# Input projection of a hybrid attention layer: seven block products in place of eight, rotated channels gathered, weight sums on GpSimd

## The reference, cut to what matters

```python
u = rms_norm(h, pre_norm)                       # (4096, 1024)
proj = einsum('bsd,de->bse', u, w_in)           # w_in: (1024, 3072)
qa, ka, va, ga, qb, kb, vb, gb, qc, gc = split(proj)   # 384,128,128,384, 384,384,384,384, 256,256
qa, ka, qb, kb = rope(...)                      # only the first 16 of each head's 64 channels are rotated
oa = banded_attention(qa, ka, va, sink)         # window 128
ob = three dilated attentions over qb, kb, vb, combined
oc = attention of qc over 256 memory tokens; their keys and values = rms_norm(mem, mem_norm) @ w_mem_kv
y  = concat(oa*silu(ga), ob*silu(gb), oc*silu(gc)) @ w_out
h  = h + rms_norm(y, post_norm)
```

## Time and profile before

| | |
|---|---|
| three runs | 2332.77, 2340.96, 2333.12 us; median 2333.12 |
| span of the profiled execution | 2347.5 us (no time of its own is given beside the span) |
| TensorE busy / VectorE / ScalarE / GpSimd, over the span | 94% / 62% / 51% / 1% |
| first and last matmul of the projection | 57.46 and 1181.96 us |
| first matmul of the attention stage | 1185.67 us |
| HBM traffic | 228 MB read, 131 MB written |

### The profile page before, as it was taken

How to read it: one execution, slowest core, us unless ns; L and a number is a source line. 1 busy time by engine, 2 the same in 40 slices (tenths; PEclk the granted TensorE clock), 3 DMA queues, 4 the chain that set the end, 5 groups by cost and what they waited for, 6 DMA issues and landing times. The chain is left out here.

```text
span 2347.5 us, 41538 instructions
## 1 busy us (share of the span) xinstructions
PE 2209.0 (94%) x13452; PEld 1846.3 (79%) x13452; DVE 1460.4 (62%) x4335; ACT 1208.0 (51%) x3198; POOL 26.3 (1%) x44
## 2 busy tenths in 40 slices
PE   5999999999999999999989999999999888899998
PEld 4888778877888778887878888888777777678886
DVE  4661237603365134641158898888889877788886
ACT  4212551225412353122279899788689878633332
POOL 0000000000000001000100000000000000000000
PEclk9999999999999999999979899899899989999999
DMA  5346434554345545448557867775869876355543
GB/s 189 130 151 186 133 113 143 169 159 140 107 147 171 155 141 192 144 158 232 155 112 132 162 122 138 138 146 113 161 134 214 200 174 184 118 165 169 167 161 125
DMA packets 394645, 361.08 MB, mean 154 GB/s; under 512 B 199120, under 2 KB 324176, under 8 KB 389504
## 3 DMA queue, kind: packets, MB, share of 16 engines
q1 hardware_dynamic: 389648, 337.51, 54.1%
q0 software_dynamic: 4848, 21.71, 3.0%
HBM read 228.34 MB, written 130.81 MB: 153 GB/s over the span
## 5 line engine op out<-in xcount | busy, mean ns | idle before, releaser
L61 PE MATMUL p_ps<-p_uT_hi,p_w_hi 128*128 128x512 f32 x1536 | 603.1, 393 | 2.5 <-DVE p_w_lo L395 2.5
L62 PE MATMUL p_ps<-p_uT_lo,p_w_hi 128*128 128x512 f32 x1536 | 599.3, 390 | 0.0
L63 PE MATMUL p_ps<-p_uT_hi,p_w_lo 128*128 128x512 f32 x1536 | 599.0, 390 | 0.0
L1265 ACT ACTIVATE probs<-probs,a_stat 128x256 f32<-128x256 f32 (+1 forms) x896 | 433.3, 489 | 52.6 <-DVE a_stat L1099 49.4
L395 DVE TENSOR_TENSOR p_w_lo<-p_w_raw,p_w_hi 128x1024 fp32r<-128x1024 f32 x96 | 117.7, 1226 | 382.6 <-ACT p_w_hi L292 363.6
L61 PEld LDWEIGHTS p_ps<-p_uT_hi,p_w_hi 128*128 128x128 f32 x1536 | 289.6, 189 | 62.8 <-issue 2.9
L63 PEld LDWEIGHTS p_ps<-p_uT_hi,p_w_lo 128*128 128x128 f32 x1536 | 289.2, 188 | 60.3
L62 PEld LDWEIGHTS p_ps<-p_uT_lo,p_w_hi 128*128 128x128 f32 x1536 | 289.3, 188 | 59.2
L1099 DVE CUSTOM_DVE_ANT_0 probs<-a_ps_s,fixed 128x256 f32<-128x256 f32 (+1 forms) x704 | 251.3, 396 | 115.1 <-PE a_ps_s L998 112.6
L1052 PE MATMUL a_ps_o<-a_pT,a_v 128*64 128x128 f32 x3320 | 264.1, 291 | 23.5 <-ACT a_pT L1289 22.0
L1068 PE MATMUL a_ps_t<-fixed,probs 128*128 128x128 f32 x1660 | 266.7, 283 | 6.2 <-ACT a_pT L1289 4.3
(11 more groups left out here) (167 smaller groups left out, 2689.2 us busy)
## 6 DMA issues: line engine op xcount, KB each, us to landing
p_w_raw<-in_w_in SPq DMA_DIRECT2D x96, 512.0 KB, 4.0
scratch_qk_hi<-p_o_hi SPq DMA_DIRECT2D x96, 256.0 KB, 2.0
scratch_qk_lo<-p_o_lo SPq DMA_DIRECT2D x96, 256.0 KB, 2.4
a_v<-scratch_v SPq DMA_DIRECT2D x40, 512.0 KB, 7.4
p_x<-in_x SPq DMA_DIRECT2D x32, 512.0 KB, 4.0
scratch_v<-p_o_v SPq DMA_DIRECT2D x256, 64.0 KB, 2.0
scratch_gate<-p_rot SPq DMA_DIRECT2D x64, 256.0 KB, 2.3
a_gate<-scratch_gate SPq DMA_DIRECT2D x64, 256.0 KB, 5.4
```

Source lines behind the costliest of these rows:

```text
L61: nc.tensor.matmul(out, w_hi, m_hi, start=first, stop=False)
L62: nc.tensor.matmul(out, w_hi, m_lo, start=False, stop=False)
L63: return nc.tensor.matmul(out, w_lo, m_hi, start=False, stop=last)
L1265: last = nc.scalar.activation(place, place, ACT.Exp, scale=-1.0, bias=stat[:, s, 0, u.column:u.column + 1], accum_out=stat[:, s, 1, u.colu ...
```

## The change

The projection is now cut in 12 groups per quarter, 48 in all (`PAIRS`). A group is a 2x2 block product: two tiles of 128 channels by two chunks of 512 tokens, with K in two halves of 512. One level of Strassen's scheme, in Winograd's form, makes its four output blocks from 7 products of 4 slices of K by 3 passes, 12 matmuls each, where 8 of that size were needed before. For this

- the token side needs four sums per quarter of 128x2048 (`add_u`), and seven splits in high and low (`high_u`, `low_u`, 128x2048 each) in place of the split of each transposed tile. There is one set of `u_hi` and `u_lo`, which is rewritten while the last group of a quarter still runs;
- the weight side needs four sums per group (`w_added`). GpSimd computes them in the first quarter, they are stored in HBM (`w_s`) and loaded from there in the later ones. Each of the seven blocks of 128x512 is split on ScalarE and VectorE two products ahead (`high_w`, `low_w`), in every quarter;
- of the output side, ScalarE copies two products per group (L477, L482) and VectorE adds twice (`join`); the rest is added up in PSUM. There are 6 banks, three for each of two groups in turn.

The channels are gathered anew: one group (R) and the half of another (L) hold all rotated channels, three groups (P) only plain channels of the same heads, and one (C) the memory queries, two (V) values and four (G) gates. The rows in HBM are as before. The tiles of the next quarter are transposed in groups 2 to 9 of a quarter; ScalarE scales a tile by its root, and the gain is multiplied in while VectorE copies the transposed tile (`keep`). The memory's keys and values are computed inside quarter 3, in its groups 1 to 5. All loops are written out.

```diff
-ORDER = ROPE_TILES + PLAIN_TILES + V_TILES + GATE_TILES
+PAIRS = (("G", 0), ("R", 0), ("G", 1), ("P", 0), ("P", 1), ("P", 2), ("L", 0), ("C", 0), ("V", 0), ("V", 1), ("G", 2), ("G", 3))
...
+        ACT_AT = {"G": (4, 5, 6, 7), "C": (4, 5, 6, 7), "P": (4, 5, 6, 7), "L": (7, 5, 10, 7), "R": (7, 9, 12, 14), "V": (6, 7, 8, 9)}
+        DVE_AT = {"C": (5, 6, 7, 8), "P": (5, 6, 7, 8), "L": (7, 6, 11, 9), "R": (8, 10, 13, 15)}
...
+        def claim_a(eng, n):
+            if n >= 4:
+                g, block = A_AT[n - 4]
+                eng.wait_ge(a_stored[n % 4], stored_before(A_AT, n, 4))
...
+                def high_w(m):                    # ScalarE
+                    g, j = divmod(m, NJ)
+                    if g < NP and j in (1, 2, 4, 5):
+                        act.wait_ge(w_added, 4 * g + {1: 1, 2: 2, 4: 3, 5: 4}[j])
...
+                    if m >= 3:
+                        act.wait_ge(multiplied, m - 2)
+                    nc.scalar.activation(w_hi[:, m % 3, :, :], w_raw[:, entry(j, g), :, :], ACT.Copy).then_inc(w_hi_ready, 1)
...
+                def slot(g, j):                   # ScalarE
+                        if j == 1:
+                            act.wait_ge(multiplied, NJ * g + 1)
...
+                            nc.scalar.activation(ps[:, 3 * (g % 2) + 2, :], ps[:, 3 * (g % 2), :], ACT.Copy).then_inc(products_copied, 1)
...
+                        high_w(m + 2)
+                    if i == NP - 1 and quarter < 3 and j > 0:
+                        high_u(quarter + 1, j - 1)
...
+                keep(XT - 1, front_bank(XT - 1))  # VectorE, ahead of the first group
+                for n in range(3):
+                    add_u(0, n)
+                for j in range(1, NJ):
+                    low_u(0, j)
+                    if j == 3:
+                        add_u(0, 3)
...
+                def slot(g, j):                   # VectorE
+                    if g < G:
+                        if j == 3:
+                            join(g, 0)
+                        if j == 5:
+                            join(g, 1)
+                        low_w(NJ * g + j + 2)
...
+                    if quarter < 3 and i == NP - 2 and j in (1, 2):
+                        add_u(quarter + 1, j - 1)
+                    if quarter < 3 and i == NP - 1 and j > 0:
+                        low_u(quarter + 1, j - 1)
+                        if j == 1:
+                            add_u(quarter + 1, 2)
+                        if j == 4:
+                            add_u(quarter + 1, 3)
...
+                def product(g, j):                # TensorE
+                    if i == 0:
+                        pe.wait_ge(u_lo_ready, NJ * quarter + j + 1)
+                    pe.wait_ge(w_lo_ready, m + 1)
...
+                    if j in (2, 3):
+                        pe.wait_ge(products_copied, 2 * g + 1)
+                    if j in (4, 5):
+                        pe.wait_ge(joined, 2 * g + 1)
+                    if j == 6:
+                        pe.wait_ge(joined, 2 * g + 2)
...
+                for g in range(NP):               # GpSimd
+                    nc.gpsimd.tensor_tensor(s1, a21, a22, ALU.add).then_inc(w_added, 1)
+                    nc.gpsimd.tensor_tensor(s2, s1, a11, ALU.subtract).then_inc(w_added, 1)
+                    nc.gpsimd.tensor_tensor(a21, a11, a21, ALU.subtract).then_inc(w_added, 1)
+                    nc.gpsimd.tensor_tensor(s4, a12, s2, ALU.subtract).then_inc(w_added, 1)
```

More of the change, by code:

```diff
@@ L55 @@
 FIXED = 12 * P
[L56 to L63, removed]
+SWAP = [*range(8, 16), *range(8), *range(24, 32), *range(16, 24)]
 def project_stage(nc, io, sc, early, ahead):
@@ L91, in project_stage @@
[L91 to L101, removed]
+        KH = KD // 2
@@ L114, in project_stage @@
[L114 to L119, removed]
@@ L127, in project_stage @@
[L127 to L138, removed]
@@ L140, in pairs @@
[L140 to L161, removed]
@@ new lines, in project_stage, with numbers @@
+        COPY_AT = {"11": 4, "12": 6, "21": 7}
+        BANK = (0, 1, 2, 0, 2, 1, 2)
+        BANK_OF = {"11": 0, "12": 1, "21": 2}
+        def numbers(place):
+            found = []
+            for g in range(G):
+                for n, block in enumerate(BLOCKS):
+                    at = place(g, n, block)
+                    if at is not None:
+                        found.append((7 * g + at, g, n, block))
+            return {(g, block): order for order, (_, g, _, block) in enumerate(sorted(found))}
@@ new lines, in project_stage, with entry, loads_of, slots @@
+        V_COPIES = lambda g, block: COPY_NO[g, block] + 1
+        def entry(j, g):
+            return j if j < 6 else 6 + g % 2
+        def loads_of(j, g):
+            if j in (1, 2, 5):
+                return g - NP + 1
+            return g // 2 + 1 if j == 6 else g + 1
+        def slots(body):
+            for g in range(G):
+                for j in range(NJ):
+                    body(g, j)
+        def due(g, j, when):
+            for age in (2, 1, 0):
+                if 0 <= g - age < G:
+                    kind = kind_of(g - age)
+                    for n, block in enumerate(BLOCKS):
+                        if kind in when and when[kind][n] == j + NJ * age:
+                            yield g - age, block
@@ L168, in project_stage, with front_bank @@
+        def front_bank(t):
+            place = (0, 1, 2, 0, 2, 0, 2, 0)[t]
+            return ps_t[:] if place == 0 else ps[:, 3 * (place - 1):3 * (place - 1) + 2, :]
         with nc.Block() as block:
@@ L373, in _, with low_w @@
+                slots(slot)
+                for j in range(3):
+                    slot(G, j)
             @block.vector
             def _(dve):
-                def normalise(quarter, t, b):
-                    n = quarter * XT + t
+                def low_w(m):
+                    if m >= NJ * G:
+                        return
+                    g, j = divmod(m, NJ)
+                    dve.wait_ge(w_hi_ready, m + 1)
+                    nc.vector.tensor_tensor(w_lo[:, m % 3, :, :], w_raw[:, entry(j, g), :, :], w_hi[:, m % 3, :, :].bitcast(F32),
+                                            ALU.subtract).then_inc(w_lo_ready, 1)
@@ L500, in _ @@
+                slots(slot)
+                for j in range(2):
+                    slot(G, j)
             @block.tensor
             def _(pe):
-                pe.wait_ge(consts, 32)
-                def turn(quarter, t, b):
-                    n = quarter * XT + t
-                    pe.wait_ge(u_ready, n + 1)
-                    if not isinstance(n, int) or n >= 2:
-                        pe.wait_ge(uT_lo_ready, n - 1)
+                pe.wait_ge(consts, 48)
+                for par in range(2):
+                    for n in range(CHUNK // P):
+                        nc.tensor.matmul(ps[:, 3 * par + 2, n * P:(n + 1) * P], ident[:], ident[:], start=n == 0, stop=n == 3,
+                                         skip_group_check=True)
@@ new lines, in turn_v @@
+                def turn_v(g, block):
+                    n = V_NO[g, block]
+                    if block == "22":
+                        pe.wait_ge(joined, 2 * g + 2)
+                        src = c22[:]
+                    else:
+                        pe.wait_ge(v_copied, COPY_NO[g, block] + 1)
+                        src = out_b[:, B_NO[g, block] % 2, :]
+                    if n >= 2:
+                        of = next(key for key, value in V_NO.items() if value == n - 2)
+                        pe.wait_ge(a_ready, A_NO[of] + 1)
+                    if g < 3 * NP:
+                        pe.wait_ge(raw_ready, XT * (g // NP + 1) + g % NP - X_AT + 1)
+                    else:
+                        pe.wait_ge(m_ready, 3)
+                    for t in range(CHUNK // P):
+                        last = nc.tensor.transpose(ps_t[:, n % 2, t * P:(t + 1) * P], src[:, t * P:(t + 1) * P], ident[:])
+                    last.then_inc(v_turned, 1)
```

1051 lines of the change are left out of this document (642 added, 409 removed).

## The result

The changed kernel takes 2366.78 us (median of 4 runs, 2361.82 to 2374.93), the kernel before 2332.94 us (4 runs, 2324.92 to 2340.96): a ratio of 1.0127, 95% interval 1.0077 to 1.0176. It is 1.3% slower, clear of the noise, where 2255 us was forecast.

What follows compares the result with a forecast made beforehand. TensorE, busy 94%, was taken as the projection's bound. Terms -130.6 + 16.9 + 0 - 20 - 3 + 26 + 21 + 9 + 3 = -77.7 took 2333.1 to 2255 us; range 2235 to 2280, eight in ten 2218 to 2295.

Steps and rivals of the forecast that it cites:

- Where VectorE is late: Projection: late joins from a quarter's last group into the next, +21 us (9 to 35); rope and plain groups, 3.
- list of what would show it wrong: TensorE waiting for `w_lo` in ordinary groups, ScalarE waiting for `w_added`, or an attention stage taking another time.
- Products: Projection: 4032 matmuls instead of 4608, 576 fewer at 0.2267 us each, -130.6 us.
- Front: Before the regular run: first product at 37.5 us, third at 61.1; net 0, between -8 and +8 us.
- The value ring: Quarter ends: SyncE late storing values, so gates wait for the ring of four buffers; +26 us, between 0 and 52.
- The joins: Last group of quarters 0 to 2: products 4 and 6 wait for VectorE's joins, 3.4 + 3.6 us, three times: +21.
- Clock: After each stop of about 3 us, some eight matmuls at 0.43 us; three stops per boundary, +9 us.
- Transposes: Projection: 24 token tiles at 1.35 us with present stalls gone, -20 us; 32 single value transposes at about 0.65, -3.
- GpSimd's sums: Quarter 0: 48 sums of 128x512 at 1.3 us each; up to about 4 us per sum costs 0.
- the second: Rival: VectorE late in ordinary groups too, 1 us in each of 48 groups, +48, 2303 us; chance 0.13.
- The loss: Rival: a TensorE hole before each of 336 products, at 0.4 us each 2389 us; chance 0.04.
- SyncE did not keep up: Rival that SyncE keeps up with the value stores, the ring never stalling: -110, 2223 us; chance 0.25.

Runs made afterwards that it cites:

- The 32x4 shape alone: Changed kernel with rows inside each head reordered so R and P tile stores walk 32x4x512 and L half stores 16x4x512; 2272.55 us, single run.
- the fastest version: Changed kernel with 32x4x512 stores (L halves 16x4x512) and four of each value block's nine stores issued by GpSimd; 2242.78 us, ratio 0.9585 to the kernel before.
- both cures: Changed kernel with stores walking 16x8x512 and four buffers in out_b instead of two (sine table left out); 2260.56 us.
- plain stores: Changed kernel with every store of queries and keys as one plain 128x512 block, the gather's scatter left out; 2273.26 us.

## Why the prediction was wrong

*The step that failed* is "Where VectorE is late", in its part on the rope and plain groups: the forecast added up VectorE's own work per slot, found it inside the slot of cover and put 3 us for all of them. Stores it costed by SyncE's issue alone, at 0; a landing, 2.1 us after the 2.0 of before, entered only for values. That the q and k stores change their shape, and that VectorE has to wait for them in a ring of two, had no term. Measured, that wait costs 108 us in groups 3 to 8 (143 less 35). The 32x4 shape alone, with nothing else changed, gives 2272.6 us, 66 below the kernel before timed beside it, where the forecast had 78. The forecast's list of what would show it wrong did not hold this wait either.

*Products* held: the matmuls run at the spacing of before, with the same median distance of 0.227 us, and there are 576 fewer. The 130.6 us are there in every version; what differs is how much the waits take back.

*Front*: forecast first product near 38, third 61.1; measured 35.4 and

```profile
60.12 0.77 PE L807 MATMUL p_ps<-p_u_hi,p_w_hi 128*128 128x512 f32 x1 [9.27 <-DVE p_w_lo L539]
```

*The value ring*: right in place and cause, too small in size. Behind the last value group of quarter 3, in the kernel after:

```profile
1191.63 0.60 ACT L444 ACTIVATE p_out_a<-p_ps 128x512 f32<-128x512 f32 x1 [15.84 <-DMA scratch_v<-p_out_a]
...
1195.67 0.77 PE L807 MATMUL p_ps<-p_u_hi,p_w_hi 128*128 128x512 f32 x1 [14.74 <-ACT p_ps L477]
```

The last groups have 66 us, 25 with GpSimd's help: 41 for the 26 forecast. By quarter that is 9.5, 4.6, 6.2 and 20.2 for 7.5, 5.7, 5.7 and 7: the miss is in quarter 3, where ScalarE waits for the stores at one place after another.

*The joins*: with the value ring out of the way, quarters 0 to 2 keep 7.7 us each in their last group, 23 for the forecast 21. In the fastest version, in quarter 1, the two waits forecast at 3.4 and 3.6:

```profile
560.64 0.47 PE L813 MATMUL p_ps<-p_u_hi,p_w_hi 128*128 128x512 f32 x1 [2.88 <-DVE p_ps L696]
...
569.04 0.47 PE L813 MATMUL p_ps<-p_u_hi,p_w_hi 128*128 128x512 f32 x1 [2.68 <-DVE p_c L701]
```

*Clock*: too small by its cause, more stops. 169 product distances of the kernel after lie between 0.33 and 0.5 us (16 in the kernel before), at 0.2 each 34 us for the forecast 9 + 1.7; in the fastest version 98. These are part of the sums above and not another cause.

*Transposes* were put too high: groups 2 to 10 of quarter 1, with both cures, hold 11.4 us of excess for 8 token tiles and 8 blocks of values, where the forecast has 8 x 1.35 + 8 x 0.65 = 16. In three quarters that is an estimate of some 14 us less, which hid as much of the misses; that is luck.

*GpSimd's sums*: 1.3 us taken, 1.33 to 1.54 measured by line, and ScalarE waits for them 13 us in all.

*The rivals.* VectorE was late in ordinary groups, as the second said, but by waiting for stores, not by its load; where the stores land in time, VectorE keeps up. The loss came by holes of 1.5 to 16 us at 35 places, not by 0.23 us in front of each product; the time lies between the forecast and the 2389 of that rival, which is chance. SyncE did not keep up in any quarter of the kernel after.

Left open: why plain stores of `scratch_qk_lo` land after 3.8 us in this kernel for 2.4 before, and 32x4 ones after 3.6, but 2.3 when SyncE waits between them. The DMA share from 300 to 1000 us rises from 0.45 to 0.60, so traffic is the likely cause; no run took it away alone.

## What to carry to other kernels

When a change gathers rows from elsewhere, read the new shape of each store as a DMA sees it: the outermost count, and next to it how long after the store its buffer is written again. A row of the page whose landing time disappears is a warning that some store on its semaphore, perhaps another row's, makes fewer than 16 updates. And a shallow ring must be costed with the landing of the new shape under the new traffic, since the engine that fills it will be late for everything in its program, here for a mean that another engine's transposes wait for.

## What the hardware showed

GpSimd's sums slow VectorE where both of VectorE's inputs are in SBUF. Timeline of quarter 0, kernel after:

```profile
84.40 0.69 DVE L539 TENSOR_TENSOR p_w_lo<-p_w_raw,p_w_hi 128x512 fp32r<-128x512 f32 x1
...
86.97 1.29 POOL L888 TENSOR_TENSOR p_w_raw<-p_w_raw 128x512 f32<-128x512 f32 x1
...
87.12 1.69 DVE L539 TENSOR_TENSOR p_w_lo<-p_w_raw,p_w_hi 128x512 fp32r<-128x512 f32 x1 [2.03 <-ACT p_w_hi L403]
...
88.22 1.75 POOL L889 TENSOR_TENSOR p_w_raw<-p_w_raw 128x512 f32<-128x512 f32 x1
```

Alone this split takes 0.69 us (58 cases between 60 and 340 us). Of the 19 that overlap a sum, 15 take longer, 0.80 to 1.78, and the sum goes from 1.29 to 1.75. VectorE's joins, with one input in PSUM, keep 0.67 to 0.70 beside a sum (10 of 10). The Trainium skill (GPSIMD Engine Reference, section "Key points") names contention with VectorE's operations on two SBUF inputs, and the trace agrees; over that stretch 77 splits take 63.0 us, some 10 us more than at 0.69 each. No wait of TensorE could be put down to it.
